# Feed-forward stage, first pair of units: the block sums on VectorE instead of GpSimd, low parts ahead of the sums of the second half's weights

## What is computed

```python
h = rmsnorm(x, pre_ffn_norm)
f = (silu(h @ w_gate) * (h @ w_up)) @ w_down      # FF = 2816 = 11 pairs of 256 hidden units
x = x + rmsnorm(f, post_ffn_norm)
```

## Time and profile before

| | before |
|---|---|
| median of three runs | 2433.16 us |
| the profiled execution | 2432.06 us |
| its span | 2430.1 us |
| TensorE busy | 2321.0 us, 96% of the span |
| VectorE busy | 1606.0 us, 66% |
| ScalarE busy | 1151.5 us, 47% |
| GpSimd busy | 429.9 us, 18% |
| mean granted TensorE clock | 0.991 of full |

### The profile page before, as it was taken

How to read it: one execution, slowest core, us unless ns; L and a number is a source line. 1 busy time by engine, 2 the same in 40 slices (tenths; PEclk the granted TensorE clock), 3 DMA queues, 4 the chain that set the end, 5 groups by cost and what they waited for, 6 DMA issues and landing times. The chain is left out here.

```text
span 2430.1 us, 33434 instructions
## 1 busy us (share of the span) xinstructions
PE 2321.0 (96%) x11448; PEld 1928.1 (79%) x11448; DVE 1606.0 (66%) x2188; ACT 1151.5 (47%) x2072; POOL 429.9 (18%) x409
## 2 busy tenths in 40 slices
PE   7999999999999999999999899997999999999997
PEld 6888888877788878887877788886887888888886
DVE  4656656565675545657687777874578777775556
ACT  4767778677633321233444455544333332334444
POOL 0323423233200000001232344540002000000000
PEclk9999999999999999999999999998999999999999
DMA  3111111010133254423332422202224444438754
GB/s 138 35 35 63 38 52 52 28 60 27 70 112 126 92 225 165 155 105 120 102 107 87 154 79 65 70 21 96 104 96 166 167 164 158 157 130 294 229 182 173
DMA packets 102620, 273.32 MB, mean 112 GB/s; under 512 B 9356, under 2 KB 35180, under 8 KB 98028
## 3 DMA queue, kind: packets, MB, share of 16 engines
q1 hardware_dynamic: 102508, 271.88, 31.9%
HBM read 196.03 MB, written 75.81 MB: 112 GB/s over the span
## 5 line engine op out<-in xcount | busy, mean ns | idle before, releaser
L53 PE MATMUL psG<-h_hi,w_hi 128*128 128x512 f32 x864 | 217.3, 394 | 3.2 <-DVE features_T L1819 1.6
L53 PE MATMUL psG<-h_hi,w_lo 128*128 128x512 f32 x864 | 215.1, 391 | 0.0
L53 PE MATMUL psG<-h_lo,w_hi 128*128 128x512 f32 x864 | 214.4, 390 | 0.0
L53 PEld LDWEIGHTS psG<-h_hi,w_hi 128*128 128x128 f32 x864 | 161.7, 190 | 39.1 <-issue 3.3
L53 PEld LDWEIGHTS psG<-h_lo,w_hi 128*128 128x128 f32 x864 | 161.5, 188 | 33.3
L53 PEld LDWEIGHTS psG<-h_hi,w_lo 128*128 128x128 f32 x864 | 161.3, 188 | 33.3
L83 DVE TENSOR_TENSOR w_lo<-w_raw,w_hi 128x1024 fp32r<-128x1024 f32 x62 | 80.3, 1297 | 84.9 <-ACT w_hi L78 84.6
L78 ACT CAST w_hi<-w_raw 128x1024 fp32r<-128x1024 f32 x64 | 67.0, 1049 | 121.5 <-PE psG L53 71.0
L376 POOL TENSOR_TENSOR sb_later_lo<-sb_later,sb_later_hi 128x512 fp32r<-128x512 f32 (+3 forms) x80 | 90.2, 1128 | 167.4 <-ACT sb_later_hi L405 167.4
L1966 POOL TENSOR_TENSOR features_T<-m_bias_both 128x512 f32<-128x512 f32 x10 | 15.9, 1593 | 539.1 <-DMA m_bias_both<-in_proj_pairs 491.8
L540 DVE SCALAR_TENSOR_TENSOR sb_sp<-psA,sb_tmp 128x128 f32<-128x128 f32 (+2 forms) x96 | 53.4, 557 | 73.7 <-ACT sb_tmp L394 73.0
(11 more groups left out here) (627 smaller groups left out, 6175.8 us busy)
## 6 DMA issues: line engine op xcount, KB each, us to landing
w_raw<-in_units SPq DMA_DIRECT2D x100, 512.0 KB, 3.5
w_raw<-hidden_blocks SPq DMA_DIRECT2D x77, 256.0 KB, 2.8
merge_gates<-features_T SPq DMA_DIRECT2D x12, 1024.0 KB, 7.7
merge_gates<-merge_gates SPq DMA_DIRECT2D x12, 1024.0 KB, 4.8
features<-features_T SPq DMA_DIRECT2D x24, 512.0 KB, 3.8
w_spare<-in_units SPq DMA_DIRECT2D x22, 512.0 KB, 4.2
hidden_blocks<-features_T SPq DMA_DIRECT2D x11, 1024.0 KB, 3.9
down_sums<-w_spare SPq DMA_DIRECT2D x22, 512.0 KB, 3.3
```

The costliest lines, as they stand in the source:

```text
L53: return pe.matmul(out, lhs, rhs, start=first, stop=last, skip_group_check=True)
```

## The change

The `gpsimd` block of this stage is removed. Its eight sums are made by VectorE within `half_pair(1, 1, 0)`, that is during the second half of pair 1 (`first` in the diff). The two waits of VectorE for those sums at the end of pair 1 go. In `first_half`, `sum3` and `sum1` of the up weights move ahead of `c22`, `low(0)` goes between the two multiplications, and `sum2` follows the multiplications, behind a wait for VectorE's own `low(6)`.

```diff
@@ first_half (VectorE)
                 low(5, 0, 1, 0)
+                after = (1, 1, 0)
+                sum3(*after)
+                sum1(*after)
                 dve.wait_ge(turned_done, TURNED0 + 14)
                 c22(0, 1, 0)
                 low(6, 0, 1, 0)
@@
                     TT(hid[0][:, r, :], hid[0][:, r, :], Y[r][:], ALU.mult).then_inc(mul, 1)
-                after = (1, 1, 0)
-                for s in (sum3, sum1, sum2):
-                    s(*after)
-                for q in range(3):
+                    if r == 0:
+                        low(0, *after)
+                dve.wait_ge(a_lo_done, count(7, 0, 1, 0, 7))
+                sum2(*after)
+                for q in range(1, 3):
                     low(q, *after)
                 c21(0, 1, 0)
@@ half_pair (VectorE), with first = kind == 1 and n == 1 and isinstance(i, int)
+                if first:
+                    own_sum(3, 0, 0)
+                    own_sum(1, 0, 0)
                 two(*cur)
                 if more:
                     low(1, *after)
+                if first:
+                    own_sum(2, 0, 0)
+                    own_sum(4, 0, 0)
...
                 if kind:
                     c11(n, i)
+                if first:
+                    down_sum(1, 0, 0)
+                    down_sum(3, 0, 0)
                 if more:
                     low(4, *after)
                     sum4(*after)
+                if first:
+                    down_sum(2, 0, 0)
+                    down_sum(4, 0, 0)
...
@@ pair (VectorE)
-                if n == 1:
-                    dve.wait_ge(own_done, 4)
-                    dve.wait_ge(dw_sum, 4)
@@ the gpsimd block, removed
-            pool.wait_ge(dw_here[0], 32)
-            TT(down_block(0, 0), down_block(0, 1), down_block(0, 0), ALU.subtract).then_inc(dw_sum, 1)
...
-            pool.wait_ge(turned_done, TURNED0 + 12)
-            pool.wait_ge(mul, 2)
-            TT(own[1], own_block(0, 0), own_block(0, 1), ALU.subtract).then_inc(own_done, 1)
...
```

More of the change, by code:

```diff
@@ L3236, in half_pair @@
                         down_sum(t, LAST, 0)
+                first = kind == 1 and n == 1 and isinstance(i, int)
+                if first:
+                    own_sum(3, 0, 0)
+                    own_sum(1, 0, 0)
                 two(*cur)
```

## The result

Ten runs of the kernel after have a median of 2441.91 us (2439.08 to 2444.83); the ten runs of the kernel before, the three of the prediction among them, have 2435.64 (2432.81 to 2437.86). The ratio of after to before is 1.0027, 95% interval 1.0019 to 1.0035: **slower by some 6 us, between 4.6 and 8.5**. The time lies 0.9 us above the range of the prediction. The profiled execution took 2441.65 us, its span is 2439.7.

What follows compares the result with a forecast made beforehand. TensorE alone was taken to bound this stage. A late transfer (2.8 us) and the clock (2.2) gave +5.0 on the profiled 2432.06, and 0.4 for the median made 2437.5 us, range 2432.5 to 2441.0.

Steps and rivals of the forecast that it cites:

- wait at q = 5 of that half: First up half: TensorE newly waits 1.3 us for VectorE's `three`, at no extra cost beside the late transfer.
- up weights there: Sync queue: pair 2's up weights land at 1871.6, 7.96 us after the down weights' load is issued.
- lost to the clock: After TensorE's 6.9 us wait, the lowered clock costs 2.2 us.
- shift of the stretch: Total delay of +5.0 us: 2.8 from the late transfer and 2.2 from the clock.
- the second wait: Next gate half, q = 5: TensorE waits 6.9 us, until 1878.6, because the up weights come late.
- the terms 2.3 and 3.0: Clock losses in us estimated from its return 4.6 and 6.1 us after the first matmul following other idle times.
- the bounds: Limits set on the clock loss after TensorE's 6.9 us wait: 1.0 and 3.2 us.
- held by nothing but the queue's own transfers: Sync queue of before: loads of down and up weights, issued at 1852.98 and 1853.84, wait only for earlier transfers there.
- The forecast of no measurable change: Whole kernel: 4.3 us above the median, below the 4.9 that can be told; chance of the same 0.48.
- the shared bandwidth: First rival's mechanism: pair 3's gate load delays the up weights by 2.6 us, giving 2440.1; chance 0.12.
- the clock and the landing at their upper ends: First rival's heading: at TensorE's 6.9 us wait, both cost their most, slower by more than 0.2%; chance 0.12.
- The second and third rivals: Up weights in time: second keeps only the 1.3 us wait, 2428.4, chance 0.10; third has neither wait, 2427.1, chance 0.06.

Runs made afterwards that it cites:

- Experiment 1: Kernel after with pair 2's up-weight load issued ahead of the hidden spill and the down-sum store; 2433.19 us, ratio to before 0.9986.
- experiment 2: Kernel after with the four own sums of the first up half behind `three` instead of around `two`; 2441.82 us, ratio to before 1.0030.
- experiment 3: Kernel after with both the early up-weight load and the own sums behind `three`; 2432.20 us, ratio to before 0.9977.
- experiment 7: Kernel after with early up-weight load, own sums behind `three`, and the old order of `first_half`; 2428.79 us, ratio to before 0.9969.
- experiment 6: Kernel after with the four down sums back on GpSimd, own sums still on VectorE; 2440.79 us, ratio to before 1.0016.
- experiment 5: Kernel before with only the new order of `first_half`, all eight sums left on GpSimd; 2433.49 us, ratio to before 0.9988.
- `before_again2`: Kernel before, unchanged, profiled a third time; one run of 2438.75 us.
- `after_again2`: Kernel after, unchanged, profiled again, second of three repeats; one run of 2436.57 us.
- experiment 4: Kernel after with the sync queue waiting for pair 2's up weights to land before issuing pair 3's gate weights; one run of 2444.2 us.
- `after_again1`: Kernel after, unchanged, profiled again, first of three repeats; one run of 2438.82 us.

## Why the prediction was right and wrong

**Right: the mechanism, step by step.** All counted from the first gate product of pair 1 (1818.46 in the prediction):

| step | predicted | after |
|---|---|---|
| first up product | 19.29 | 19.42 |
| wait at q = 5 of that half | 1.3 | 1.05 |
| next gate half | 39.6 | 39.95 |
| down weights' load issued | 45.1 | 45.06 |
| up weights there | 53.1 | 53.49 |
| wait of TensorE | 6.9 | 6.86 |
| TensorE resumes | 60.1 | 60.57 |
| lost to the clock | 2.2 | 1.6 |
| shift of the stretch | +5.0 | +4.9 |

Experiment 1 takes the second wait away alone, experiment 2 shows the first to be free beside it, experiments 3 and 7 show that nothing else is lost.

That the sum agrees to 0.1 us is in part luck. The up weights were there 0.47 us later after the down weights' issue than predicted (8.43 against 7.96), and the clock cost 0.6 us less; the two cancel. The 0.47 is a slip of the working: 7.1 is the landing of the second of the two issues, which starts half a microsecond after the first, and the prediction counted it from the first. The traces of before and after both give 7.1. In the windows from 1680 and 1383 the clock is 0.74 and 0.72, so it came back about half way in each, and the terms 2.3 and 3.0 are a little small; the bounds hold all that was measured.

One reading was wrong and did no harm to the sum. The prediction has the loads of before "held by nothing but the queue's own transfers". GpSimd's own sums ended at 1837.64 + 6.65 = 1844.29, and the sync queue of before shows the spill at once behind them:

```profile
1844.32 0.34 SPq L2834 DMA_DIRECT2D hidden_blocks<-features_T  x1
```

So the up weights hung on the own sums already, and the prediction named only the moved down sums as the cause of their lateness. In after the down sums do hold the last store; in experiment 6, with only the own sums on VectorE, the load is late too.

**Wrong: the level on which the sum was put.** This is the step that failed. The prediction's last step was to set +5.0 on the profiled execution's 2432.06 and to add 0.4, "something less than half" of the 1.1 us by which the median of three lay above; no reason stands for the halving. Those three runs were 2432.81, 2433.16 and 2436.57. The ten runs of before have 2435.64, which is 3.6 above the profiled execution where the prediction had 0.4. Over the 25 further runs of before beside which experiments 1 to 3 were measured, the median is 2436.64 (2432.14 to 2438.38), and over the 23 of experiments 5 to 7 it is 2436.88. Set on 2435.64 the same +5.0 gives 2440.6, within the range of the prediction, and on 2436.64 it gives 2441.6; measured were 2441.91. The range, which ended at 2441.0, was made of the stage's unknowns alone and had no term for how an execution reaches the stage. The forecast of no measurable change had the same fault less: at +5.0, right at the 4.9 that count as a change, the halving pushed it under, to 4.3. The medians differ by 6.3.

**Where the level comes from.** Ahead of the stage, the first profiles of the two kernels drift apart by up to 5 us: they are 0.6 us apart near 576 and 5.0 near 880. The windows view and, under it, TensorE's row behind its wait in that window, before and then after:

```profile
572.00:580.00 8.00, 5.41 (x25) 4.22 (x24) 4.79 (x8) 7.42 (x15) 1.53 (x1) 1.00 0.19 66
...
575.87 0.50 PE L705 MATMUL psA<-sb_sp_lo,minus_from_r 128*128 128x512 f32 x1 [2.59 <-DVE sb_sp_lo L550]
```

```profile
572.00:580.00 8.00, 5.42 (x19) 4.14 (x18) 3.43 (x5) 7.13 (x12) 1.51 (x1) 0.79 0.20 66
...
576.46 0.80 PE L705 MATMUL psA<-sb_sp_lo,minus_from_r 128*128 128x512 f32 x1 [2.58 <-DVE sb_sp_lo L550]
```

TensorE has the same work and the same wait. In the windows view x25 and x19 are its matmuls, and 1.00 and 0.79 its clock. In one execution the clock stays full; in the other it falls to 1.2 GHz behind the wait, and fewer matmuls are done in the same window. The same happens near 624 and near 652 in the profile of after and not in that of before. `before_again2` shows the lower clock at the first place (0.82), `after_again2` the full one.

Over the fourteen profiles of this study that wait is 2.58 or 2.59 us long each time, and the clock falls behind it in seven. These seven are the ones that resume from it latest, at 576.18 to 577.35 us; the seven that resume at 575.47 to 576.10 keep the full clock. The former begin the stretch at 1822.5 to 1824.3, the latter at 1818.1 to 1819.1, but for one at 1822.03. So whether the clock falls goes, in these fourteen, with when the wait comes and not with the kernel: before and after each stand on both sides. I read this from the profiles afterwards and tested it with no run of its own, and 0.08 us separate the two groups. Why it is so stays open; nothing in these kernels differs there.

**The rivals.** Of the first, the shared bandwidth falls at the 2.6 us it was given (experiment 4), and "the clock and the landing at their upper ends" happens: 3.05 us of clock in experiment 4, 1.2 us of landing and 2.5 of clock in `after_again1`, whose stretch is 7.0 above before's first. The second and third rivals, no late transfer, are what experiments 1 and 3 build on purpose; it took a change of the queue to get there. The time of experiment 1 less before, -3.5 against the 25 runs, is near the -4.1 worked out for the second, and so is the stretch's -3.9.

**The rule of the Trainium skill against the change** ("DMA: Bandwidth & Descriptors", Rules for kernel authors, Overlap DMA with compute: issue early, wait late) agrees with what decided here: experiment 1 issues one load some 21 us earlier in the stretch (24.8 against 45.9) and turns the change from 5.3 us slower into 3.5 faster, both against the median of the same 25 runs (beside its own ten runs of before, after is 6.3 slower).

What stays open: the ratio 1.0027 is 6.6 us of 2436, the stretches differ by 4.9 in the first pair of profiles and by 5.1 in the mean (87.1 over four of after, 82.0 over three of before). The interval covers both, so I don't seek a further cause.

## What to carry to other kernels

When work moves from an idle engine to one with a fixed order, look past the engine's own time: ask which semaphores that work releases, which queue stands behind them and what else is in that queue. Here eight sums of 0.6 us held a load that they have nothing to do with, because it stood behind two stores in one queue. And a forecast to a few tenths of a percent needs the level as much as the shift: three runs that sit at 2433 and at 2437 are not one number, and the range has to hold that gap.

## What the runs showed of the hardware that was not expected

The cost of the clock behind a wait varies from one execution to the next: 1.5 to 3.05 us over six profiles with a wait of 6.7 to 8.2 us (6.93, 6.98, 7.03, 7.09, 7.98 and 8.49 us for two products that take 5.44). It does not go with the length of the wait: 7.09 stands behind one of 8.17 us, 8.49 behind one of 6.97. The same idle time of 2.58 or 2.59 us was followed by the full clock in seven profiles and by half the clock in seven, and a shift of under 2 us in when it ended went with which of the two it was. And the same pair of loads behind the same traffic landed 7.4 to 7.7 us after issue in four executions (`own_behind` and three of after) and 8.9 in one.
